# The two parts of the normalised input at another column in each stage, with constants allocated ahead of them

## The reference

```python
def rms_norm(x, g):
    x32 = x.astype(jnp.float32)
    y = x32 * lax.rsqrt(jnp.mean(x32 * x32, axis=-1, keepdims=True) + RMS_EPS)
    return (y * g.astype(jnp.float32)).astype(x.dtype)
...
def swiglu(h, w_in, w_out):
    g, u = jnp.split(h @ w_in, 2, axis=-1)
    return (jax.nn.silu(g) * u) @ w_out
...
def first_block(x, c, rel_bias, ...):
    c_act = jax.nn.silu(c)
    for i in range(DEPTH):                      # DEPTH = 2
        mod = (c_act @ ada_w[i] + ada_b[i])[:, None, :]
        sh_a, sc_a, g_a, sh_f, sc_f, g_f = jnp.split(mod, 6, axis=-1)
        h = rms_norm(x, norm_g[i, 0]) * (1.0 + sc_a) + sh_a
        y = moba_attention(h, ...) if i == 0 else diff_attention(h, ...)
        x = x + g_a * rms_norm(y, norm_g[i, 1])
        h = rms_norm(x, norm_g[i, 2]) * (1.0 + sc_f) + sh_f
        x = x + g_f * rms_norm(swiglu(h, ffn_w_in[i], ffn_w_out[i]), norm_g[i, 3])
    return x
...
def second_block(x, c, ...):                    # one layer, with its own modulation
    h = rmsnorm(x, norm_pre_mix[0]) * (1.0 + sc_m) + sh_m
    y = conformer_conv_module(h, ...)           # h @ w1, gate, 31 taps in depth, layer norm, silu, @ w2
    x = x + gt_m * rmsnorm(y, norm_post_mix[0])
    h = rmsnorm(x, norm_pre_ffn[0]) * (1.0 + sc_f) + sh_f
    y = conv_ffn(h, ...)                        # h @ w_up, 3 taps in depth, silu(gt) * v, @ w_down
    x = x + gt_f * rmsnorm(y, norm_post_ffn[0])
    return x
```

## Time and profile before

| | |
|---|---|
| median of 3 runs | 997.55 us (996.96 to 998.17) |
| profiled execution | 997.55 us, span 995.7 us |
| TensorE matmul / weight load busy | 963.3 us (97%) / 886.0 us (89%) |
| VectorE / ScalarE / GpSimd busy | 821.5 us (83%) / 543.3 us (55%) / 77.9 us (8%) |
| matmuls | 6806 |
| moved from HBM | 232.27 MB, 234 GB/s over the span |

### The profile page before, as it was taken

How to read it: one execution, slowest core, us unless ns; L and a number is a source line. 1 busy time by engine, 2 the same in 40 slices (tenths; PEclk the granted TensorE clock), 3 DMA queues, 4 the chain that set the end, 5 groups by cost and what they waited for, 6 DMA issues and landing times. The chain is left out here.

```text
span 995.7 us, 19019 instructions
## 1 busy us (share of the span) xinstructions
PE 963.3 (97%) x6806; PEld 886.0 (89%) x6806; DVE 821.5 (83%) x1217; ACT 543.3 (55%) x1023; POOL 77.9 (8%) x111
## 2 busy tenths in 40 slices
PE   4899999999999999998999999999999999999997
PEld 3899988999999888996999999989997899999996
DVE  4869978887777778777988777789998989987885
ACT  3455546544444467555644444459998555555452
POOL 2100002000000012011300000002240000000000
PEclk9999999999999999999999999999999999999999
DMA  9999973999999965652599999985340649766641
GB/s 347 327 339 336 337 256 108 349 348 318 312 312 310 285 190 162 179 176 79 174 354 347 317 312 308 314 258 170 86 127 1 201 133 286 225 187 183 183 121 42
DMA packets 240770, 234.08 MB, mean 235 GB/s; under 512 B 7497, under 2 KB 208970, under 8 KB 240714
## 3 DMA queue, kind: packets, MB, share of 16 engines
q1 hardware_dynamic: 237824, 226.52, 73.8%
q0 software_dynamic: 1616, 5.32, 1.6%
q10 hardware_dynamic: 1274, 1.52, 0.4%
HBM read 232.27 MB, written 1.06 MB: 234 GB/s over the span
## 5 line engine op out<-in xcount | busy, mean ns | idle before, releaser
L1341 DVE TENSOR_TENSOR wlo<-raw,whi 128x1024 fp32r<-128x1024 f32 x286 | 346.7, 1222 | 67.4 <-ACT whi L999 67.2
L527 PE MATMUL work<-h_hi,whi 128*128 128x256 f32 x1360 | 383.1, 282 | 2.0 <-DVE h_lo L1402 1.9
L527 PE MATMUL work<-h_hi,wlo 128*128 128x256 f32 x1360 | 381.0, 280 | 0.0
L527 PE MATMUL work<-h_lo,whi 128*128 128x256 f32 x1360 | 380.8, 280 | 0.0
L999 ACT ACTIVATE whi<-raw 128x1024 fp32r<-128x1024 f32 x286 | 297.7, 1053 | 143.5 <-PE work L527 45.4
L527 PEld LDWEIGHTS work<-h_hi,whi 128*128 128x128 f32 x1360 | 256.5, 189 | 5.4 <-issue 2.0
L527 PEld LDWEIGHTS work<-h_lo,whi 128*128 128x128 f32 x1360 | 256.1, 188 | 3.1
L527 PEld LDWEIGHTS work<-h_hi,wlo 128*128 128x128 f32 x1360 | 257.0, 189 | 0.0
L1351 DVE SCALAR_TENSOR_TENSOR acc<-ada_raw,csil,acc 128x1024 f32 (+1 forms) x128 | 163.7, 1280 | 6.1 <-DMA ada_raw<-in_ada_w 4.4
L564 PE MATMUL Y<-whi,ab_hi 128*128 128x512 f32 x286 | 90.0, 395 | 0.0
L564 PE MATMUL Y<-whi,ab_lo 128*128 128x512 f32 x286 | 89.8, 395 | 0.0
(11 more groups left out here) (226 smaller groups left out, 1323.8 us busy)
## 6 DMA issues: line engine op xcount, KB each, us to landing
ada_raw<-in_ada_w SPq DMA_DIRECT2D x88, 512.0 KB, 6.5
raw<-in_ffn_w_in SPq DMA_DIRECT2D x88, 512.0 KB, 7.6
ada_raw<-in_mod_w SPq DMA_DIRECT2D x48, 512.0 KB, 6.8
raw<-in_ffn_w_out SPq DMA_DIRECT2D x44, 512.0 KB, 5.7
raw<-in_f_up_w SPq DMA_DIRECT2D x44, 512.0 KB, 4.0
raw<-in_moba_w_qkv SPq DMA_DIRECT2D x24, 512.0 KB, 8.3
raw<-in_diff_w_qkv SPq DMA_DIRECT2D x24, 512.0 KB, 7.8
raw<-in_a_pw_w SPq DMA_DIRECT2D x24, 512.0 KB, 6.5
```

Of the source, the lines that this page charges most:

```text
L527: mm = pe.matmul(dst, w[:, u, ws], h[:, k, :], start=(k == 0 and m == 0), stop=(k == KT - 1 and m == 2))
L1341: dve.tensor_tensor(wlo[:, u, :], raw[:, u, :], whi[:, u, :].bitcast(F32), ALU.subtract).then_inc(lo[u], 1)
```

## The change

The four tensors csil, colA, colB and taps (176 columns, 704 bytes) are allocated ahead of h_hi instead of behind cols. h_hi and h_lo become flat tensors with 80 columns (320 bytes) to spare each. A table H_AT gives the column at which both begin in a stage, and h_at[s] holds the two views of stage s; every writer and reader of h takes the views of its stage. small is cut from 96 to 64 columns.

```diff
--- before.py
+++ after.py
@@ -57,6 +57,8 @@
 STEPS = {1: 0, 3: 22, 4: 44, 5: 52}
 HEADS = {0: 0, 2: 8}
 GATE_BANK = {0: 1, 1: 0, 2: 2, 3: 0, 4: 0, 5: 0}
+H_AT = {0: 0, 1: 48, 2: 80, 3: 64, 4: 32, 5: 16}
+H_ROOM = 80
 NI_A, NI_F, NI_C = H // 2, FT // 2, KT // 2
 
 
@@ -82,8 +84,12 @@
         acc = sb("acc", [P, 6 * D])
         xt_eps = sb("xt", [P, TT, D + 1])
         xs_pad = sb("xs", [P, TT, D + 1])
-        h_hi = sb("h_hi", [P, KT, S], F32R)
-        h_lo = sb("h_lo", [P, KT, S], F32R)
+        csil = sb("csil", [P, 16])
+        colA = sb("colA", [P, KT])
+        colB = sb("colB", [P, KT])
+        taps = sb("taps", [P, 2, 72])
+        h_hi = sb("h_hi", [P, KT * S + H_ROOM], F32R)
+        h_lo = sb("h_lo", [P, KT * S + H_ROOM], F32R)
         head_bias = sb("head_bias", [P, H, REL])
         Ga = sb("Ga", [P, D])
         Gf = sb("Gf", [P, D])
@@ -91,17 +97,15 @@
         ab_lo = sb("ab_lo", [P, 2, PADW], F32R)
         mix = sb("mix", [P, 2692])
         cols = sb("cols", [P, COLS])
-        csil = sb("csil", [P, 16])
-        colA = sb("colA", [P, KT])
-        colB = sb("colB", [P, KT])
-        taps = sb("taps", [P, 2, 72])
         ident = sb("ident", [P, P])
         ones = sb("ones", [P, P])
-        small = sb("small", [P, 96])
+        small = sb("small", [P, 64])
         relt = sb("relt", [32, H])
         Y = ctx.enter_context(nc.psum_tensor("Y", [P, 4, 512], F32))
         work = ctx.enter_context(nc.psum_tensor("work", [P, 4, 512], F32))
 
+        h_at = {s: [h[:, at:at + KT * S].rearrange("p (k n) -> p k n", k=KT) for h in (h_hi, h_lo)]
+                for s, at in H_AT.items()}
...
+            def col_product(s, dst, u, n, early=None, before=None):
+
+                hh, hl = h_at[s]
                 pe.wait_ge(lo[u], n + 1)
                 for k in range(KT):
                     if early is not None and (k % 2 == 0 or k == 1):
                         pe.wait_ge(hlo, h_parts_before(early) + (1, 2, 3, 0, 4, 0, 5)[k])
                     ws = slice(k * P, (k + 1) * P)
-                    for m, (w, h) in enumerate(((whi, h_hi), (whi, h_lo), (wlo, h_hi))):
+                    for m, (w, h) in enumerate(((whi, hh), (whi, hl), (wlo, hh))):
                         mm = pe.matmul(dst, w[:, u, ws], h[:, k, :], start=(k == 0 and m == 0),
                                        stop=(k == KT - 1 and m == 2))
                         if before is not None and k == 0 and m == 0:
@@ -532,6 +537,7 @@
...
-                    act.activation(h_hi[:, k0:k1, :], x_parts(s, k0, k1), ACT.Copy).then_inc(hhi, 1)
+                    act.activation(h_at[s][0][:, k0:k1, :], x_parts(s, k0, k1), ACT.Copy).then_inc(hhi, 1)
...
-                    dve.tensor_tensor(h_lo[:, k0:k1, :], x_parts(s, k0, k1), h_hi[:, k0:k1, :].bitcast(F32),
+                    dve.tensor_tensor(h_at[s][1][:, k0:k1, :], x_parts(s, k0, k1), h_at[s][0][:, k0:k1, :].bitcast(F32),
                                       ALU.subtract).then_inc(hlo, 1)
 
```

More of the change, by code:

```diff
@@ L518, in _ @@
         def _(pe):
-            def col_product(dst, u, n, early=None, before=None):
+            def col_product(s, dst, u, n, early=None, before=None):
+                hh, hl = h_at[s]
                 pe.wait_ge(lo[u], n + 1)
@@ L748, in values @@
                             ws = slice(k * P, (k + 1) * P)
-                            for m, (h, w) in enumerate(((h_hi, whi), (h_lo, whi), (h_hi, wlo))):
+                            for m, (h, w) in enumerate(((hh, whi), (hl, whi), (hh, wlo))):
                                 mm = pe.matmul(work[:, 1, t * S:(t + 1) * S], h[:, k, ts], w[:, 4:6, ws],
@@ L774, in step @@
                     else:
-                        col_product(work[:, 0, 0:S], j, i + nb, s if n == 0 else None, used[4] if j else None)
+                        col_product(s, work[:, 0, 0:S], j, i + nb, s if n == 0 else None, used[4] if j else None)
                         if s == 0:
@@ L779, in step @@
                             need(pe, sb_done, n * 2 + HEADS[2])
-                        col_product(work[:, 3, 0:S], 2 + j, i + nb)
+                        col_product(s, work[:, 3, 0:S], 2 + j, i + nb)
                     if n >= lag:
@@ L843, in products @@
                             pe.wait_ge(gate_done, before + fb)
-                    col_product(work[:, 2 * j, 0:S], j, i + nb)
+                    col_product(s, work[:, 2 * j, 0:S], j, i + nb)
                     if not start:
@@ L849, in products @@
                             pe.wait_ge(act_done, before + fb)
-                    col_product(work[:, 2 * j + 1, 0:S], 2 + j, i + nb)
+                    col_product(s, work[:, 2 * j + 1, 0:S], 2 + j, i + nb)
                 products(0, 0)
@@ L872, in conformer @@
             def conformer():
-                nb, fb = USE[4][0], STEPS[4]
+                s, nb, fb = 4, USE[4][0], STEPS[4]
                 def conv(i, j, half_way=None):
@@ L971, in conformer @@
                             pe.wait_ge(p_lo, k + 1 if r == 0 else r + 2)
-                            row_tile(h_hi[:, k, :], h_lo[:, k, :], 4 + 2 * (r % 2) + j,
+                            row_tile(h_at[4][0][:, k, :], h_at[4][1][:, k, :], 4 + 2 * (r % 2) + j,
                                      USE[4][2 + r % 2] + r // 2, t, end=(k == KT - 1))
@@ L1300, in conformer @@
                     hs = slice(ks[0], ks[-1] + 1)
-                    act.activation(h_hi[:, hs, :], convT[:, hs, :], ACT.Copy).then_inc(p_hi, 1)
+                    act.activation(h_at[4][0][:, hs, :], convT[:, hs, :], ACT.Copy).then_inc(p_hi, 1)
                 prep(1, NI_C + nb)
@@ L1841, in low_group @@
                     dve.wait_ge(p_hi, n + 1)
-                    dve.tensor_tensor(h_lo[:, hs, :], convT[:, hs, :], h_hi[:, hs, :].bitcast(F32),
+                    dve.tensor_tensor(h_at[4][1][:, hs, :], convT[:, hs, :], h_at[4][0][:, hs, :].bitcast(F32),
                                       ALU.subtract).then_inc(p_lo, 1)
```

## The result

The changed kernel takes 999.53 us (median of 17 runs) beside 997.55 us for the kernel before (17 runs): 1.0018 times, 95% interval 1.0012 to 1.0025. It is slower by some 1.8 us: less than the 0.2% that the prediction took as measurable, but clear of no change. The profiled execution has a span of 997.2 us, 1.5 more than before.

What follows compares the result with a forecast made beforehand. TensorE's matmul rate was taken to bound the kernel. From 997.55 us, one gated stage at the faster pace takes off 4.6, other terms at 0, giving 992.9; range 978 to 996, or 984 to 1004 for 8 in 10.

Steps and rivals of the forecast that it cites:

- What bounds the kernel: TensorE's matmul rate sets the time, busy 963.3 of 995.7 us; weight loads and splitting on other engines do not.
- case 1: Faster, chance 0.41: one of gated stages 1, 3, 5 goes from 117.9 to 113.5 ns a matmul, 4.6 us less, 992.9.
- short rhythm: Steady pace of 113.5 ns between starts of 256-column matmuls, beside 117.9; seen in stages 0 and 2 only, 384 matmuls.
- Case 3: Slower, chance 0.29: unequal distances of h's parts make products uneven, 119.5 ns; 5.1 us in gated stages, 1002.6, up to 1006.8.
- 384 short ones lost: Stages 0 and 2: the 384 matmuls at 113.5 ns lose that pace, 6.0 ns each, 2.3 us more.
- bounds of case 1: Matmuls reading h: 4.4 ns less each at best; 4.6 us for one gated stage, 19.0 us for all 4320.
- rows behind: The 512-column row matmuls, whose operands move: taken at 0, bounded with the convolution by 1.7 us either way.
- floor of 111.5 ns: 32 matmuls against ones, 128 columns: 111.5 ns from start to start, read as set by the weight load.
- Writers of h, loads and clock: Writers on ScalarE and VectorE taken at 0, 3.6 us either way at most; loads don't take the gain back; clock stays.
- Case 2: No change, chance 0.30: starts at multiples of 64 bytes are alike, entry alone sets the pace; 997.5, between 996 and 999.
- the reading offered at its end: Gated stages 1, 3, 5 should differ if distance acts; their agreeing would make the prediction wrong; no size given.

Runs made afterwards that it cites:

- the fastest kernel: Against the kernel before: one tensor for both parts of h, 48 spare columns, column 12 in stages 1, 3, 5, 0 elsewhere: 985.25 us, 0.9880.

## Why the prediction was wrong

It said 992.9 us and faster; the kernel is slower by 0.18%. The measured 999.53 is inside the range of 984 to 1004, which was drawn over all three cases and says nothing for the first.

- What bounds the kernel was right: a change of TensorE's pace alone moved the time from 985 to 1007 us, with no new wait over 1.3 us (for the activations, in the fastest kernel).
- The step that failed is case 1, that one of the three gated stages falls into the short rhythm. None did: 117.9, 117.7 and 117.9 ns. That they had "nothing of the short rhythm to lose and everything to win" was an argument from the two rhythms seen, not from a mechanism. What was missing is that the change puts the low part 64 bytes further modulo 256 than the high one in all stages: the kernel that differs in this alone has every second pair of stage 1 short (-2.2 us). But its stage 3 takes 2.2 us more at 120.0 ns and its stage 5 nothing less, so with equal parts, too, these columns would not have given 992.9; it took 999.05 us. There was something to lose. Case 3 named the inequality but priced it by the convolution's 119.5, 1.8 ns too high for the gated stages here.
- The term "384 short ones lost" had the right count and mechanism. It was priced at 6.0 ns each, 2.3 us; they went to the long rhythm and cost 4.4 to 4.5 ns each, 1.74 us. That is the size of the measured loss, some 1.8 us; the other changes cancel, by chance as far as is known.
- The bounds of case 1 were sound: one stage 4.6 us at most, and 2.8 to 3.4 us measured for column 12, because the first product of each pair needs its first matmuls to settle.
- The rows behind, taken at 0 and bounded by 1.7 us: in this kernel -0.1 us a gated stage, right. The bound was too narrow: at distance 0 they give 1.2 us a stage, 227 ns.
- The floor of 111.5 ns was read as the weight load's, and the rows don't show that. The matmuls against ones are of plain float32. The four of line 600 in the kernel before, of that type too and with 512 columns, start (1.88 - 0.592) / 3 = 0.429 us apart (0.592 is the mean duration on that line), against 0.233 for the faster form:

```profile
753.68 1.88 PE L600 MATMUL work<-acc,ones 128*128 128x512 f32 x4
```

A quarter of that, 107 ns, is already near 111.5 by the columns alone. No term of the sum used the floor.
- Writers of h, loads and clock: at nothing, right.
- Case 2's rule, that starts which are multiples of 64 bytes are alike, is refuted by 120.0 ns at distance 0 and 113.3 or 117.8 at 64. So is the reading offered at its end, that three gated stages alike mean that distance does not act: they were alike because one cause hit all.
- The runs show that the products' pace goes from 113.3 to 121.8 ns by starts alone, with the same work on every other engine. The Trainium skill (SBUF — State Buffer, "Who interferes with whom") calls TensorE's two read ports independent and says that it never waits on anyone; that section has nothing on placement, and no run here shows whether the two reads get in each other's way. Where in the chip the time is lost was not tried and stays open.

## What to carry to other kernels

Where TensorE is full and each matmul loads its own stationary tile, read the distance between starts in the timeline, not the mean: two paces for one form, 113.3 and 117.8 ns here, are room that neither busy shares nor waits show. Vary the start of one operand by a few columns per stage, so that one run tries six places, and begin with the parts of a split operand at the same start modulo 256 bytes; the best column was found by trying, and the runs give no rule for it. And compare stages, not totals: two kernels here took the same 999 us with stages that differed by 2 us each way.

## What the hardware showed that was not expected

- A matmul's start-to-start time with 256 moving columns and its own load depends on the start of h in steps of 4 bytes: 117.5 ns at distance 76, 121.3 at 72, 113.3 at 112, 121.8 at 116.
- It repeats with 256 bytes where that was tried (113.3 ns at 112 and 368, 120.0 at 0 and 256; low part 320 bytes further like 64 bytes further, 119.6 ns each).
- At some distances (64, 192) there are two steady paces, 113.3 and 117.8 ns, kept for up to 96 matmuls in a row. Moving only the operands of the other matmuls changed which stretches get which.
- The 512-column matmuls have paces of their own: they settle at 227 ns with the even row at 0 and the odd one at 120, and take 230.8 to 234 ns, averaged over 12, at the five other pairs of places tried. By the Trainium skill's N / 2.4 GHz + 2.5 ns (TensorE: Matmul & The Clock Gate, "Wait — 56ns, not 53.3ns?") it would be 215.8 ns, an estimate that no placement here came to.
